# A two-layer DiT block with 32 experts on one core: 1 MB pieces for expert 3, and a reordered start of the expert loop

## What is computed

```python
D_MODEL, SEQ, N_EXPERTS, TOP_K, D_EXPERT = 1024, 256, 32, 2, 512

def moe(h_flat, router_w, router_b, w_gate, w_up, w_down):
    experts, gates = route(h_flat, router_w, router_b)   # 2 experts for each token
    ...                                                  # tokens sorted by expert
    def expert_block(args):
        xb, e = args
        return (jax.nn.silu(xb @ w_gate[e]) * (xb @ w_up[e])) @ w_down[e]
    ...                                                  # gated sum back to the tokens
```

## Time and profile before

| | us |
|---|---|
| median of three runs | 1275.6 (1272.42 to 1276.04) |
| the profiled execution's own time | 1275.22 |
| its span | 1273.4 |

### The profile page before, as it was taken

How to read it: one execution, slowest core, us unless ns; L and a number is a source line. 1 busy time by engine, 2 the same in 40 slices (tenths; PEclk the granted TensorE clock), 3 DMA queues, 4 the chain that set the end, 5 groups by cost and what they waited for, 6 DMA issues and landing times.

```text
span 1273.4 us, 13818 instructions
## 1 busy us (share of the span) xinstructions
PE 1186.2 (93%) x5088; PEld 498.0 (39%) x5088; DVE 453.1 (36%) x952; ACT 179.8 (14%) x381; POOL 70.4 (6%) x87
## 2 busy tenths in 40 slices
PE   7999999899999999999899999999999999988888
PEld 3444445554333333333233376543333333332333
DVE  4297776667211212211211165651122112112122
ACT  2211216632000000000000021410000000000000
POOL 0013100000000000000000000000000000000000
PEclk9899999999999999999999999999999999999999
DMA  9948749479999999999999999799999999999997
GB/s 361 406 168 347 284 176 401 165 290 353 422 421 423 421 423 421 423 421 423 422 422 421 421 395 380 298 378 421 421 423 422 422 422 422 422 422 422 421 421 309
DMA packets 82187, 485.58 MB, mean 381 GB/s; under 512 B 6242, under 2 KB 7906, under 8 KB 32996
## 3 DMA queue, kind: packets, MB, share of 16 engines
q1 hardware_dynamic: 80128, 481.38, 92.6%
q10 hardware_dynamic: 2020, 3.67, 0.8%
HBM read 483.98 MB, written 1.05 MB: 381 GB/s over the span
## 4 chain that ended last, share of the span: by engine, by line
PE 54%; SPq 32%; DMA 5%; DVE 4%; ACT 3%; issue 3%; POOL 0%; ACTq 0%; DVEq 0%; POOLq 0%
SPq L339 25%; PE PS L871 16%; PE PS L667 9%; PE PS L890 8%; SPq L347 5%; PE PS L917 4%; DMA ring<-in_moe_w_down 4%; PE PS L637 2%; PE PS L741 2%; PE PS L1118 2%; PE PS L1094 2%; SPq L353 1%; DVE TMP L1897 1%; PE PS L696 1%; ACT ring L1193 1%
## 5 line engine op out<-in xcount | busy, mean ns | idle before, releaser
L871 PE MATMUL PS<-ring,KQH 128*64 128x512 f32 x2048 | 455.6, 594 | 16.9 <-DMA ring<-in_moe_w_up 15.9
L871 PEld LDWEIGHTS PS<-ring,KQH 128*64 128x64 f32 x2048 | 148.7, 137 | 309.6 <-issue 267.8
L890 PE MATMUL PS<-ring,KQH 128*64 128x512 f32 x960 | 220.9, 602 | 41.0 <-DVE TMP L1897 25.3
L1924 DVE TENSOR_TENSOR KQH<-KQH,PS 128x256 f32<-128x256 f32 x64 | 39.0, 610 | 404.9 <-ACT KQH L1335 404.5
L890 PEld LDWEIGHTS PS<-ring,KQH 128*64 128x64 f32 x960 | 66.6, 137 | 156.5 <-issue 121.2
L917 PE MATMUL PS<-TMP,KQH 128*128 128x512 f32 x256 | 126.4, 617 | 0.2
L1335 ACT ACTIVATE KQH<-PS 128x256 f32<-128x256 f32 x62 | 23.8, 384 | 681.7 <-PE PS L871 672.6
L667 PE MATMUL PS<-ring,KQH 128*128 128x512 f32 x256 | 114.0, 593 | 0.0
L1897 DVE TENSOR_TENSOR TMP<-PS,TMP 64x512 f32<-64x512 f32 x62 | 42.7, 689 | 131.1 <-PE PS L890 105.5
L1897 DVE TENSOR_TENSOR TMP<-PS,KQH 64x512 f32<-64x512 f32 x62 | 42.7, 689 | 127.6 <-PE PS L890 104.0
L498 POOL COPY KQH<-KQH 128x512 f32 x62 | 38.1, 616 | 810.7 <-PE PS L871 761.1
(11 more groups left out here) (261 smaller groups left out, 789.5 us busy)
## 6 DMA issues: line engine op xcount, KB each, us to landing
ring<-in_moe_w_gate SPq DMA_DIRECT2D x128, 1024.0 KB, 25.6
ring<-in_moe_w_up SPq DMA_DIRECT2D x128, 1024.0 KB, 26.3
ring<-in_moe_w_down SPq DMA_DIRECT2D x60, 2048.0 KB, 26.3
ring<-in_ada_w SPq DMA_DIRECT2D x23, 2048.0 KB, 14.6
ring<-in_attn_w_in SPq DMA_DIRECT2D x2, 4096.0 KB, 12.8
ring<-in_moe_w_down SPq DMA_DIRECT2D x8, 1024.0 KB, 27.1
ring<-in_attn_w_in SPq DMA_DIRECT2D x2, 2048.0 KB, 21.4
ring<-in_attn_w_out SPq DMA_DIRECT2D x1, 4096.0 KB, 24.1
```

Source lines behind the costliest of these rows:

```text
L871: ins = mm(PS[64 * f:64 * f + 64, 4, :], xs[:, k, 0:SLOTS], gu_w[s][:, :, k, 256 * f:256 * f + 256], start=k == 0, stop=k == KC - 1)
L890: ins = mm(PS[64 * f:64 * f + 64, b, :], lhs, dn_w[s][:, c, 512 * f:512 * f + 512], start=c == 0, stop=c == 3)
```

## The change

It edits the start of each layer's expert stage; the loops and all sizes of computation stay.

- Loads: expert 3 comes as four gate+up pieces of 1 MB (two transfers of 0.5 MB each, lines of 4 KB) and two down pieces of 1 MB; expert 4's first gate+up part comes as two pieces of 1 MB. The new semaphore `early_free` releases one piece of each pair in the middle of the product that reads its slot. Experts 4 (the rest) and 5 are written out ahead of SP's loop. `early_in` counts the early pieces, and `gate_up_first` waits for it where c is 3.
- PE, first gather: chunk 7 is gathered after the products of chunks 4 and 5. Second gather: chunks 0 to 2, transposes, chunks 3 and 4, the first half of expert 0's down product, chunks 5 to 7, the second half.
- DVE: one spread stands between the two halves of `pick`; `gates` comes after `hidden(1)` and a spread. ACT: the copy of the transposes comes one spread earlier.

```diff
-            b = ((5, 6, 7, 3), (6, 7, 3, 2))[half][k % 4]
+            b = ((5, 6, 7, 3, 5, 6, 7, 3), (6, 7, 3, 2, 7, 3, 2, 7))[half][k]
...
+            def load_fourth(L, s):
+                for part in range(2):
+                    for j in range(2):
+                        if j == 0:
+                            sp.wait_ge(early_free, 4 * L.l + part + 1)
+                        else:
+                            sp.wait_ge((L.gu_half, L.gu_done)[part], 1)
+                        k = 4 * part + 2 * j
+                        for a, w in enumerate((w_gate, w_up)):
+                            sp.dma_start(gu_w[s][:, a, k:k + 2, :], w[L.l, 3].rearrange("(p k) f -> p k f", p=P)[:, k:k + 2, :]
+                                         ).then_inc((L.gu_in, L.gu2_in)[part][s] if j else early_in, 16)
+                for a in range(2):
+                    if a == 0:
+                        sp.wait_ge(early_free, 4 * L.l + 3)
+                    else:
+                        sp.wait_ge(L.dn_done, 1)
+                    sp.dma_start(dn_rows[s][:, a], w_down[L.l, 3, 256 * a:256 * a + 256].rearrange("(p b) n -> p b n", b=2)
+                                 ).then_inc(L.dn_in[s] if a else early_in, 16)
...
+                load_fourth(L, L.slot(0))
+                for j in range(2):
+                    if j == 0:
+                        sp.wait_ge(early_free, 4 * L.l + 4)
+                    else:
+                        sp.wait_ge(L.gu_half, 2)
...
+                load_gate_up(L, 4, L.slot(4), True, (1,))
+                load_down(L, 4, L.slot(4), True)
+                load_expert(L, 5, L.slot(5), freed=True)
+                with sp.Fori(1, (NE - 5) // 3) as it:
...
+                if c == 3:
+                    pe.wait_ge(early_in, 112 * L.l + 112)
...
+                for k in (4, 5, 6):
+                    later_chunk(k)
                 pe.wait_ge(L.gu2_in[L.slot(0)], 32)
+                later_gate_up(4)
+                later_gate_up(5).then_inc(early_free, 1)
+                later_chunk(7)
+                later_gate_up(6)
+                later_gate_up(7).then_inc(L.gu_done, 1)
...
-                spread(L, 1, 3)
                 act.wait_ge(L.tr_done, 1)
                 nc.scalar.copy(t_sb[:, 256:512], PS[:, 5, 256:512]).then_inc(L.t_ready, 1)
-                for k in range(5, KC, 2):
+                for k in range(3, KC, 2):
                     spread(L, 1, k)
...
                 first_places(L)
-                gates()
...
                 hidden(1)
-                for k in range(0, KC, 2):
+                spread_v(L, 1, 0)
+                gates()
+                for k in range(2, KC, 2):
                     spread_v(L, 1, k)
                 dve.wait_ge(xg_done, 16 * L.l + 2 * KC)
                 V.memset(HT[:, 0:SLOTS], 0.0).then_inc(xs_v, 1)
```

More of the change, by code:

```diff
@@ L302, in program @@
         end_first = sem("end_first")
+        early_free, early_in = sem("early_free"), sem("early_in")
         end_bank = (7, 5)
@@ L331, in rows_of, with load_gate_up @@
                 return w.rearrange("(k p) n -> p k n", p=P)[:, :, c0:c0 + n]
-            def load_gate_up(L, e, s, freed):
-                for part in range(2):
+            def load_gate_up(L, e, s, freed, parts=range(2)):
+                for part in parts:
                     if freed:
@@ L425, in _ @@
             for L in layers:
-                with sp.Fori(0, (NE - 5) // 3) as it:
+                load_fourth(L, L.slot(0))
[4 more added lines that the diff above has]
+                        sp.wait_ge(L.gu_half, 2)
+                    for a, w in enumerate((w_gate, w_up)):
+                        sp.dma_start(gu_w[L.slot(4)][:, a, 2 * j:2 * j + 2, :],
+                                     w[L.l, 4].rearrange("(p k) f -> p k f", p=P)[:, 2 * j:2 * j + 2, :]
+                                     ).then_inc(L.gu_in[L.slot(4)] if j else early_in, 16)
+                load_gate_up(L, 4, L.slot(4), True, (1,))
+                load_down(L, 4, L.slot(4), True)
+                load_expert(L, 5, L.slot(5), freed=True)
+                with sp.Fori(1, (NE - 5) // 3) as it:
                     for c in range(3):
@@ L986, in experts, with later_chunk @@
                     ins = gate_up(L.slot(0), dense, [k])
+                    if k == 1:
+                        ins.then_inc(early_free, 1)
                 ins.then_inc(L.gu_half, 1)
                 pe.wait_ge(lo_ready, 4 * L.l + 4)
-                for k in range(4, KC):
+                def later_chunk(k):
                     for t in range(NT):
@@ L1005, in experts @@
                 transposes(None).then_inc(L.tr_done, 1)
[L1006 to L1008 removed]
+                pe.wait_ge(slots_known, L.l + 1)
+                second_places(L, 3)
+                pe.wait_ge(xs_a, 8 * L.l + 5)
+                second_places(L, 4)
                 pe.wait_ge(L.t_ready, 1)
[L1010 to L1013 removed]
+                pe.wait_ge(xs_v, 9 * L.l + 5)
+                pe.wait_ge(L.dn_in[L.slot(0)], 16)
+                down_half(L.slot(0), 0, t_sb, 6).then_inc(early_free, 1)
+                pe.wait_ge(xs_v, 9 * L.l + 6)
+                second_places(L, 5)
+                pe.wait_ge(xs_a, 8 * L.l + 6)
+                second_places(L, 6)
+                pe.wait_ge(xs_v, 9 * L.l + 7)
+                second_places(L, 7)
+                down_half(L.slot(0), 1, t_sb, 6).then_inc(L.dn_done, 1)
+                pe.wait_ge(L.gu_in[L.slot(1)], 32)
+                pe.wait_ge(L.xw_ready, 1)
+                gate_up(L.slot(1), xw[1], range(2)).then_inc(early_free, 1)
+                gate_up(L.slot(1), xw[1], range(2, 4)).then_inc(L.gu_half, 1)
                 gate_up_second(L, 1, 1, 0)
@@ L1909, in experts @@
             def experts(L):
-                pick(L, dpos)
+                for t in range(NT):
+                    pick_first(dpos, t)
+                    pick_second(dpos, t)
                 low_parts(L, 1, 0)
@@ L1914, in experts @@
                 link(V.tensor_scalar(dpos2, dpos, -float(HALF), None, ALU.add))
-                for k in range(4, KC):
+                for k in (4, 5, 6):
                     spread_v(L, 0, k)
-                pick(L, dpos2)
+                for t in range(NT):
+                    pick_first(dpos2, t)
+                spread_v(L, 0, 7)
+                for t in range(NT):
+                    pick_second(dpos2, t)
                 first_places(L)
-                gates()
                 def hidden(n):
```

21 lines of the change are left out of this document (9 added, 12 removed).

## The result

The change makes the kernel slightly slower: 1275.88 us median (1274.18 to 1279.37) against 1273.46 (1272.31 to 1276.04) for the kernel before on the same chip. The ratio of the interleaved runs is 1.0015, interval [1.0009, 1.0021], so about 1.9 us, with an interval of 1.1 to 2.7 us. The forecast was -0.15 us. The time lies inside the stated range, but the forecast's "The holes move; the end does not." did not hold.

What follows compares the result with a forecast made beforehand. Each layer's end was taken as set by when the DMA engines stay full, plus bytes left. Layer 0 +0.05 and layer 1 -0.2 gave -0.15 us, 1275.1 against the profiled 1275.22, or 1275.5 by medians; range 1272.0 to 1279.0.

Steps and rivals of the forecast that it cites:

- The holes move; the end does not.: Conclusion on both layers: DMA idle time only shifts to ahead of expert 4's down load; -0.15 us in all.
- What bounds the kernel: Each layer's expert stage: its end is set by when the DMA engines are full without a break, plus bytes left.
- PE late at expert 1's down product: Later gather end delays the memset 2.2 us, hence `hidden(2)`; PE late 1.6 us in layer 0, 1.35 in layer 1.
- the rival of a stall there: Second gather waits for DVE at the transposes or chunk 5: 1279.6 us, chance 0.09; less of it, 1276.5 to 1279, 0.14.
- the rival of small transfers paid in series: Seven more transfers a layer each pay a fixed 2.0 us, 14 us a layer: near 1298 us, chance 0.01.
- Layer 1: Sum for the second layer's expert stage: PE 1.35 us late less 1.57 slack, -0.2 us.
- the cap: Expert 4's down load can start only 1.56 us earlier on an empty queue; this slack limits each layer's gain.
- Layer 0: Sum for the first layer's expert stage: PE 1.6 us late less 1.56 slack, +0.05 us.
- C: Follow-up theory, not the forecast's: PE's lateness alone is the loss, the clock a bystander, slack smaller than 1.56 us.
- The hole of 180 GB/s: DMA idle time at 294 to 298 us in layer 0, 2.3 us lost; expert 3's earlier first piece closes it.
- the new hole: DMA idle time of 1.6 to 1.8 us ahead of expert 4's down load, swallowing 0.4 us from slower 4 KB lines.
- The switch from PE to SP's queue about one expert earlier: Sign that the forecast is right: in the chain of waits, SP's queue takes over from PE about one expert sooner.

Runs made afterwards that it cites:

- e_busy2: Kernel before with two products without use on PE after the routing wait, both layers: 1273.96 us, ratio 1.0000 to the kernel before.
- e_busy4: Kernel before with four products without use on PE after the routing wait, both layers: 1277.68 us, ratio 1.0024 to the kernel before.
- e_pieces: Changed kernel's loads in pieces with early releases, but PE, DVE and ACT in the order of the kernel before: 1273.29 us, ratio 0.9990 to before.
- e_after: The changed kernel itself run once more, nothing altered: 1276.29 us, ratio 1.0014 to the kernel before.
- e_order: Changed kernel's order on PE, DVE and ACT with the loads of the kernel before: 1277.05 us, ratio 1.0025 to before.
- e_dvelate: Kernel before with ten linked copies more on DVE, so that `hidden(2)` is late and PE waits: 1275.19 us, ratio 1.0013 to before.
- e_warm: Changed kernel with one product without use on PE ahead of the routing wait, both layers: 1275.52 us, ratio 1.0007 to the kernel before.
- e_warm_b: Second run of the changed kernel with one product without use ahead of PE's routing wait: 1275.49 us, ratio 1.0005 to the kernel before.
- e_pieces4: Pieces in the order of before, with expert 4's down load also in two halves, the first released early: 1271.18 us, ratio 0.9981 to before.
- e_warm4: Changed kernel with the product without use on PE and expert 4's down load in two halves: 1273.34 us, ratio 0.9992 to the kernel before.

## Why the prediction was right or wrong

**What bounds the kernel: right.** The DMA engines are full from expert 4 on in both kernels. PE's delays cost only where they release a load late beyond its slack (by bytes, e_busy2: 0.1 to 0.2 of 1.2 us; e_busy4: 1.3 to 2.0 of 2.94).

**PE late at expert 1's down product: right in place, cause and size.** The memset came 304.57 - 288.53 = 16.04 us after the start of the stage (before 13.67), 2.4 us later; 2.2 was forecast. The product came 1.65 us late in layer 0 (1.6 forecast) and 1.43 in layer 1 (1.35). Expert 1's gate and up product began 0.66 us late (17.66 against 17.00 after the start), where 0.4 was reckoned. There was no new wait in the second gather, so the rival of a stall there did not occur. Nor did the rival of small transfers paid in series (near 1298): e_pieces has the same seven more transfers a layer and was not slower than before.

**Layer 1: right in its number, in part by luck.** Forecast -0.2, by bytes -0.2 (e_after: 0.0). The number is the difference of two terms, and both were too large (see the cap, below).

**Layer 0: wrong, and this is the failed step: PE's lateness taken as a shift without a price for the clock.** The forecast was 1.6 late less 1.56 slack, +0.05; it came to +1.7 by bytes. The sum took PE's lateness as a pure shift, with every product as long as before ("that costs nothing by itself"). But lateness of this kind is a wait, 1.28 us in place of 0.28, and behind it the down product ran at 0.51 of the clock, 1.70 us longer. The release of expert 4's down load was then 3.35 us late against a slack of 1.56: 1.8 us, measured 1.7. The sum has no term for it: it asks how long the wait is, not what the engine does behind it, and none of its rows has this product at the lower clock. Shown: the half clock in layer 0 in all four profiles in which PE waits 1.28 us or more there (after, e_after, e_order, e_dvelate) and in none of the other ten, where that wait is 0.46 us or less or does not occur, while in layer 1 waits of 1.04 to 1.36 us left the clock whole in the same four; the loss by bytes vanishes when the clock is kept up (e_warm, e_warm_b) and appears when only the wait is added (e_dvelate). Not shown: that it is all of the timed loss. By the ratios e_warm is 1.0 us below after and e_warm_b 1.1 below e_after, which ran beside it, of 1.8 to 1.9; both stay 0.5 to 0.7 parts in a thousand above before, with intervals from below 1 to 1.0016, so the rest is either scatter of the last engine or some tenths of C. The three executions without the half clock that were not faster point the same way. That stays open.

**The cap: right in kind, too high in size, and so was the charge for lateness.** With PE on time the forecast had up to 1.56 us a layer. e_pieces got 0.6 and 0.4. What was not charged is the slow stretch behind the dry moment (0.9 and 1.5 us in the two windows); with the next load split as well, so that the queue does not run dry, the same pieces gave 1.2 and 0.9. The prediction also takes one microsecond off for each microsecond of PE's lateness. With the pieces there and the clock whole, the new order, with PE late by 1.7 and 1.4 us, cost 0.5 and 0.4 us of bytes (e_pieces to e_warm; to e_warm_b 0.7 and 0.0), and with the split load 0.5 and nothing (e_pieces4 to e_warm4). The new order also issues expert 3's first down piece 1.1 us earlier, so that this is not the price of the lateness alone. So the +0.05 and -0.2 of the sum are met where the clock is whole (e_warm -0.1 and 0.0), but as the difference of a cap and a charge that are both about 1 us too large. Another term was too good: the pieces were reckoned at 410 GB/s, from the ada_w rows. Windows of after that hold mostly pieces:

```profile
293.00:297.00 4.00, 4.00 (x23) 1.82 (x22) 2.57 (x7) 0.00 (x0) 0.00 (x0) 1.00 0.96 332
297.00:302.00 5.00, 5.00 (x34) 3.42 (x34) 4.31 (x16) 1.89 (x4) 0.00 (x0) 1.00 1.00 350
```

Engines at a share of 0.96 and 1.00, and 332 and 350 GB/s. The hole of 180 GB/s was filled, with less than was reckoned. That the new hole swallows this in after, as forecast, no run isolates; whether the rate is due to the line length or to the small gathers' traffic beside it is not settled.

**The signs.** DMA busy across the first hole, smaller holes near expert 0's down product, the new hole ahead of expert 4's down load, the wait for DVE: all seen. Issue of that load "near 323.2" is 322.38 + 2.57 = 324.95 on before's clock, off by the 1.70. "The switch from PE to SP's queue about one expert earlier" was wrong: the chain of waits of after

```profile
524.10 3.45 PE PS L905 x16
527.71 5.37 SPq L340
```

switches at 527.71 - 288.53 = 239 us after the start, before at 500.41 - 291.10 = 209. PE is later, so it lives on the stock longer. As a sign it is weak: e_pieces and e_pieces4, whose PE runs alike, differ by two experts in it, for less than 1 us of bytes.

## What to carry to other kernels

When an edit makes TensorE wait, price two things: the shift, and what its clock may do in the work behind the wait; the length of the wait alone did not tell here whether it falls. If that work releases a load, its lengthening counts as lateness, and a microsecond of useless products in the wait can be cheaper. Slack reckoned from mean bytes was an upper bound here: behind a dry moment the DMA queue can take some microseconds to come back, so a load pulled forward wants its successor pulled forward too. And a net forecast near zero that is right does not show that its two terms are.

## What the runs showed of the hardware that was not expected

- After a wait of 1.28 us (with 0.86 us more some 0.6 us later), TensorE's granted clock was 0.51 for 3.4 us, and a product of 3.65 us took 5.35. In layer 1, after 1.05 us and the same 0.86, it stayed at 1.00, and so it did in layer 1 of e_dvelate after 1.36 and 0.95 us, and late in layer 0 of after behind waits of 1.31 us. In layer 0 it came in 4 of 4 profiles with such a wait, and in 0 of 10 without; by the mean clocks of their 51 executions it came in most, not in all.
- Behind a dry moment, e_pieces' queue moved 349 and 315 GB/s over 5 and 6 us, at a DMA share of 0.94 and 0.91, before it reached 422. Behind a deeper hole in after it moved 451 GB/s within 3 us of the issue.
- The last landing of a layer scatters by about 2 us between two executions of one kernel (e_warm +0.2, e_warm_b +2.0) at equal bytes in the first 50 us. Which engine lags, and why, was not found out.
